# A hybrid state-space, attention and expert layer: the state-space group in chunks of four tokens, both token groups at once, weights read once

## What is computed

```python
sh1, sc1, g1, sh2, sc2, g2 = modulation(cvec, w_mod, b_mod)      # silu(c) @ w_mod, 12 pieces of 512
h = modulate(x, norm1, sh1, sc1)
u, c_q, c_kv, k_rope = split(h @ w_in)                            # 512, 384, 256, 32
# S5 group: 32 groups of 16 channels and 64 complex states, forward and backward
#   h_t = A h_{t-1} + B u_t   (A diagonal),   y_t = D u_t + Re(C h_t)
ssm_out, ssm_state = s5_mixer(u)          # gelu(y) * sigmoid(gelu(y) @ w_glu)
attn = attend(q, k, v)                    # 8 heads; group 1 also sees the cached latents
x = x + g1 * (concat([ssm_out, attn]) @ w_out)
h2 = modulate(x, norm2, sh2, sc2)
# experts: 8 heads, top 16 of 128 x 128 keys each -> 128 picks of 16384 rows per token
act = gelu(einsum('nd,nhkd->nhk', h2, u_table[idx])) * softmax(best)
x = x + g2 * einsum('nhk,nhkd->nd', act, v_table[idx])
```

## Time and profile before

| | |
|---|---|
| median of 3 runs | 947.65 us (945.67 to 949.99) |
| profiled execution, whole | 953.76 us |
| its span, first to last instruction | 952.0 us |
| TensorE, VectorE, ScalarE, POOL busy | 761.3, 632.1, 267.0, 427.5 us |
| mean granted TensorE clock | 0.896 of 2.4 GHz |
| moved by DMA | 339.02 MB, 356 GB/s over the span |

### The profile page before, as it was taken

The page is one execution under the profiler, slowest core; times in us unless marked ns, Lnnn a source line. Parts: engine busy times, 40 slices in busy tenths (PEclk is TensorE's granted clock), DMA queues, the critical chain, the costliest instruction groups (busy, mean ns, idle before and its releaser), DMA issues. The chain is left out here.

```text
span 952.0 us, 9512 instructions
## 1 busy us (share of the span) xinstructions
PE 761.3 (80%) x3129; PEld 396.9 (42%) x3129; DVE 632.1 (66%) x1327; ACT 267.0 (28%) x836; POOL 427.5 (45%) x380
## 2 busy tenths in 40 slices
PE   4798869656688999979998788876786888787885
PEld 0474534544344664336665533332332333333331
DVE  7689975684779737475853478469649756845453
ACT  3334451011245531213132224223222221311220
POOL 1058972556433344154344154653543635354520
PEclk9889789768799999989999898997988989788997
DMA  9937682067799999999999999999999999999991
GB/s 381 405 143 314 268 304 79 5 236 256 296 393 399 364 423 421 403 386 390 420 421 420 421 422 412 421 423 421 421 422 421 396 421 422 364 423 422 421 421 42
DMA packets 48250, 339.02 MB, mean 356 GB/s; under 512 B 5628, under 2 KB 6076, under 8 KB 8392
## 3 DMA queue, kind: packets, MB, share of 16 engines
q0 software_dynamic: 36864, 268.45, 68.8%
q1 hardware_dynamic: 10968, 69.78, 18.4%
q10 hardware_dynamic: 368, 0.18, 0.1%
HBM read 337.16 MB, written 1.23 MB: 355 GB/s over the span
## 5 line engine op out<-in xcount | busy, mean ns | idle before, releaser
L618 PE MATMUL psum<-mem 128*128 128x512 f32 x1024 | 489.8, 636 | 107.9 <-ACT mem L955 107.9
L1197 POOL DMA_INDIRECT mem<-uv_table,small x256 | 304.2, 1188 | 382.4 <-PE psum L618 330.8
L1504 DVE CUSTOM_DVE_ANT_0 mem<-mem,h 128x1024 f32<-128x1024 f32 x256 | 307.2, 1225 | 201.6 <-DMA mem<-uv_table,small 199.7
L618 PEld LDWEIGHTS psum<-mem 128*128 128x128 f32 x1024 | 205.1, 204 | 379.6 <-issue 253.4
L943 ACT ACTIVATE small<-small 128x4 f32<-128x4 f32 x64 | 13.1, 205 | 396.1 <-DVE small L1504 396.0
L955 ACT ACTIVATE mem<-consts,small 128x128 f32<-128x128 f32 x256 | 80.8, 386 | 0.0
L597 PEld LDWEIGHTS psum<-hT,mem 128*128 128x128 f32 x512 | 63.2, 205 | 4.2 <-issue 3.1
L597 PE MATMUL psum<-hT,mem 128*128 128x128 f32 x512 | 63.6, 289 | 0.7 <-issue 0.7
L1172 POOL TENSOR_TENSOR mem<-mem 128x512 f32<-128x512 f32 x32 | 46.1, 1460 | 39.7 <-DVE mem L1356 39.7
L1159 POOL TENSOR_TENSOR mem<-mem 128x512 f32<-128x512 f32 x32 | 50.1, 1574 | 22.3 <-DVE mem L1342 22.3
L948 ACT ACTIVATE small<-small 128x1 f32<-128x1 f32 x256 | 54.5, 283 | 5.9
(11 more groups left out here) (158 smaller groups left out, 604.5 us busy)
## 6 DMA issues: line engine op xcount, KB each, us to landing
mem<-w_mod SPq DMA_DIRECT2D x24, 1024.0 KB, 11.7
mem<-w_query SPq DMA_DIRECT2D x14, 1024.0 KB, 9.2
mem<-w_out SPq DMA_DIRECT2D x8, 1024.0 KB, 9.2
mem<-uv_table,small POOLq DMA_INDIRECT x256, 13.3
mem<-w_in_qkv SPq DMA_DIRECT2D x4, 1008.0 KB, 11.2
mem<-w_uq SPq DMA_DIRECT2D x4, 576.0 KB, 5.9
mem<-w_in_u SPq DMA_DIRECT2D x2, 1024.0 KB, 16.5
mem<-w_ukv SPq DMA_DIRECT2D x2, 1024.0 KB, 9.5
```

The source lines that it names most:

```text
L618: mm = pe.matmul(bank(f"acc_{g}_{half}"), diag[:, pick % DEEP, :], rows[pick % ROWS][:, D + 512 * half:D + 512 * half + 512], start=first ...
L1197: pool.indirect_dma_start(rows[row], None, uv_table, bass.IndirectOffsetOnAxis(ap=idx[:, pick:pick + 1], axis=0)).then_inc(row_landed[row] ...
L1504: dve.tensor_tensor_reduce(out=row[:, 0:D], in0=row[:, 0:D], in1=h[:, it // NB, :], scale=1.0, scalar=0.0, op0=ALU.mult, op1=ALU.add, accu ...
```

## The change

The state-space group is cut into chunks of four tokens. With powers of A multiplied into B and C beforehand (`xpow`, `ypow`), four tokens by 16 channels make a vector of 64: the input of 32 chunk states is one matmul 64 x 64 per block (`s5_in`), the scan runs over 33 steps instead of 128 (one is the initial state), and the output is the carried part (`y_carried`) plus what the chunk's own tokens give (`y_local`, with Toeplitz matrices from `kernels` and `toeplitz`). `shifted` brings tokens into chunk form, `y_spread` back. A unit now holds both groups, both directions and a quarter of the channels: 528 elements a partition, 4 units.

Both token groups now go through gate, projection inputs and latents together, and attention of group 1 up to its scores stands before the expert loop. qkv, glu, out and all query pages are sent once; uq and ukv twice as before. Modulation is sent by steps of 128 rows, and its last quarter (g2) in the expert loop. Rows are handed out by `row_plan`: four pages at first, a fifth from pick 4, seven from pick 6, nine from pick 25, eleven from pick 89.

```diff
-UN = 2 * NC
+STEP = 4
+CHUNKS = P // STEP
+SL = CHUNKS + 1
...
+PAGES = [(f"mod0.{k}", (0, 1, 2, 3, 4, 5, 0, 1)[k]) for k in range(8)]
+PAGES += [("in_u.0", 2), ("in_u.1", 3), ("qkv.0", 4), ("qkv.1", 5), ("qkv.2", 0), ("uq.0", 1), ("uq.1", 6), ("ukv", 7)]
+PAGES += [(f"mod1.{k}", (2, 3, 4, 5, 0, 2, 3, 4)[k]) for k in range(8)]
+PAGES += [("glu", 5), ("out0.0", 0), ("out0.1", 1), ("out1.0", 6), ("out1.1", 7)]
+PAGES += [(f"mod2a.{i}", (2, 3, 4, 2)[i]) for i in range(4)]
+PAGES += [("uq2.0", 3), ("uq2.1", 4), ("ukv2", 12), ("query0.0", 2), ("query0.1", 5), ("query1.0", 3), ("query1.1", 4),
+          ("query2.0", 2), ("query2.1", 5), ("query3.0", 3), ("query3.1", 4)]
+PAGES += [(f"mod2b.{i}", (2, 5, 2, 5)[i]) for i in range(4)]
...
+def row_plan():
+    free, arriving = [13, 14, 8, 9], {4: 15, 5: 0, 6: 1, 24: 6, 25: 7, 88: 3, 89: 4}
...
+        work = [mem[:, at_:at_ + WORK].rearrange("p (k n) -> p k n", k=4) for at_ in (Z0, Z0 + WORK, WIN0)]
+        BUF = (0, 1, 2, 0)
...
+            sp.wait_ge(coef_used, 1)
+            load("uq.1")
+            load("ukv")
+            for n in range(ORDER["mod1.0"], ORDER["uq2.0"]):
+                load(PAGES[n][0])
+                if PAGES[n][0] == "mod1.1":
+                    wait_filled(sp, "W_3_1")
+                    sp.wait_ge(x0_ready, 1)
+                    sp.dma_start(att[1].ckvn[:, 0, :], cache_ckv).then_inc(cache_in, 16)
+            load("uq2.0")
+            load("uq2.1")
+            sp.wait_ge(y_ready, NC)
+            sp.wait_ge(last_ready, 2 * NC)
+            load("ukv2")
+            sp.dma_start(n2b[0], norm2.to_broadcast([P, D])).then_inc(n2_in, 16)
+            sp.dma_start(page(10), keys).then_inc(keys_in, 16)
+            for name in ("query0.0", "query0.1", "query1.0", "query1.1"):
+                load(name)
+            wait_filled(sp, "mix_1_1")
+            sp.dma_start(n2b[1], norm2.to_broadcast([P, D])).then_inc(n2_in, 16)
+            for n in range(ORDER["query2.0"], len(PAGES)):
...
+            def input_weights(c):
+                if c == 0:
+                    pe.wait_ge(xpow_ready, 1)
+                for r in range(2):
+                    out = start(f"W_{c}_{r}")
+                    for a in range(8):
+                        for e in range(2):
+                            es = slice(64 * e, 64 * e + 64)
+                            mm = pe.matmul(out[es, 64 * a:64 * a + 64], xpow[es, r, 8 * c + a, :, :].rearrange("p k q -> p (k q)"),
+                                           ident[es, es], start=True, stop=True, tile_position=(64 * e, 64 * e))
...
+            def shifted(out, c, moving):
+                for j in range(4):
+                    for low in range(2):
+                        for e in range(2):
+                            for high in range(2):
+                                q = 64 * e + 32 * high
+                                mm = pe.matmul(out[q:q + 32, 64 * j:64 * j + 64], pad[:, 2 * j + e, 16 - 16 * low:48 - 16 * low],
+                                               moving(2 * high + low), start=low == 0, stop=low == 1, tile_position=(0, q))
+                return mm
...
+            def kernels():
...
+                for c in range(NC):
+                    for d, at_, lo, hi in ((0, 3, 0, 4), (1, 0, 2, 5), (1, 3, 5, 6)):
+                        for r in range(2):
+                            for j in range(4):
+                                a, o_ = 8 * c + 4 * d + j, 112 * c + SP_ * at_
+                                mm = pe.matmul(out[32 * j:32 * j + 32, o_:o_ + SP_ * (hi - lo)], x0[:, a, r, :],
+                                               ypow[:, r, a, lo:hi, :].rearrange("p k q -> p (k q)"),
+                                               start=c == 0 and d == 0 and r == 0, stop=c == NC - 1 and lo == 5 and r == 1,
+                                               tile_position=(0, 32 * j))
...
+            def toeplitz(half):
...
+                for c in range(2 * half, 2 * half + 2):
+                    mm = shifted(out[:, 256 * (c % 2):256 * (c % 2) + 256], c, lambda s: kern[:, c, 16 * (3 - s):16 * (3 - s) + 64])
+                finish(mm, f"m_{half}")
+
...
             def s5_in(u):
-                g, v = u // UN, u % UN
-                c, d = v // 2, v % 2
+                wait_emptied(pe, f"W_{u}_0")
+                wait_emptied(pe, f"W_{u}_1")
+                wait_emptied(pe, f"Us_{u}")
                 if u:
                     pe.wait_ge(bu_used, u)
                 for r in range(2):
-                    for j in range(4):
-                        mm = pe.matmul(psum[:, j, P * r:P * r + P],
-                                       fbT[32 * j:32 * j + 32, UN * r + v, :], tokens(uT[32 * j:32 * j + 32, g, c, :], d),
-                                       start=True, stop=True, tile_position=(32 * j, 0))
+                    for a in range(8):
+                        d, j = a // 4, a % 4
+                        for e in range(2):
+                            es = slice(64 * e, 64 * e + 64)
+                            mm = pe.matmul(psum[es, r, 64 * a:64 * a + 64], win[es, u, r, a, :],
+                                           chunks(ut[es, u, j, :].rearrange("p (g n) -> p g n", g=G), d),
+                                           start=True, stop=True, tile_position=(64 * e, 64 * e))
                 mm.then_inc(bu_ready, 1)
 
-            def s5_out(u):
-                g, v = u // UN, u % UN
-                c, d = v // 2, v % 2
+            def y_local(u):
+                wait_emptied(pe, f"m_{u // 2}")
+                if u >= 2:
+                    pe.wait_ge(y_read, u - 1)
+                out = psum[:, 4 + u % 2, :]
+                for j in range(4):
+                    for e in range(2):
+                        es = slice(64 * e, 64 * e + 64)
+                        pe.matmul(out[es, 64 * j:64 * j + 64], toep[es, u, j, :], ut[es, u, j, :], start=j == 0, stop=False,
+                                  tile_position=(64 * e, 64 * e))
+
+            def y_carried(u):
                 pe.wait_ge(qd_ready, 2 * u + 2)
                 pe.wait_ge(qp_ready, 2 * u + 2)
-                if u and d == 0:
-                    pe.wait_ge(y_read, u // 2)
-                for k, (r, b) in enumerate(((0, 0), (0, 2), (1, 1), (1, 3))):
+                out = psum[:, 4 + u % 2, :]
+                for j in range(4):
+                    for d in range(2):
+                        a = 4 * d + j
+                        for k, (r, b) in enumerate(((0, 0), (0, 2), (1, 1), (1, 3))):
+                            for e in range(2):
+                                es = slice(64 * e, 64 * e + 64)
+                                mm = pe.matmul(out[es, 64 * j:64 * j + 64], ypow[es, r, 8 * u + a, 1:5, :].rearrange("p k q -> p (k q)"),
+                                               chunks(view(u, b)[es, a, :, 0:CHUNKS], d),
+                                               start=False, stop=j == 3 and d == 1 and k == 3, tile_position=(64 * e, 64 * e))
+                mm.then_inc(y_ready, 1)
+
+            def y_spread(u):
+                pe.wait_ge(ysb_ready, u + 1)
+                out = psum[:, 4 + u % 2, 256:512].rearrange("p (g n t) -> p g n t", g=G, t=STEP)
+                for t in range(STEP):
                     for j in range(4):
-                        mm = pe.matmul(psum[32 * j:32 * j + 32, 4, P * c:P * c + P], cm[:, r, 4 * v + j, :],
-                                       tokens(work[:, u % 3, b, P * j:P * j + P], d),
-                                       start=d == 0 and k == 0, stop=d == 1 and k == 3, tile_position=(0, 32 * j))
-                mm.then_inc(q_used, 1)
+                        mm = pe.matmul(out[32 * j:32 * j + 32, :, :, t], phase[:, t, :],
+                                       ysb[:, u % 2, j, :], start=True, stop=True, tile_position=(0, 32 * j))
+                mm.then_inc(ysh_ready, 1)
 
...
+            def available(page_):
+                if page_ in (13, 14):
+                    pool.wait_ge(y_ready, NC)
+                    pool.wait_ge(last_ready, 2 * NC)
+                elif page_ in (8, 9):
+                    pool.wait_ge(h2_ready, 1)
+                elif page_ == 15:
+                    wait_filled(pool, "at1")
+                elif page_ in (0, 1):
+                    wait_filled(pool, f"mix_1_0")
+                elif page_ in (6, 7):
+                    pool.wait_ge(h2_ready, 2)
+                else:
+                    wait_filled(pool, "qry_1_3")
 
             def gather(pick):
-                row = pick % ROWS
                 if pick % BATCH == 0:
                     pool.wait_ge(idx_ready, pick // BATCH + 1)
-                if pick >= ROWS:
-                    pool.wait_ge(row_free, pick - ROWS + 1)
-                elif row < 2:
-                    wait_filled(pool, "mix_0_1")
-                elif row < 6:
-                    pool.wait_ge(qd_ready, 2 * UN + 4 * (row - 1))
```

(32 more changed lines are left out.)

1263 lines of the change are left out of this document (663 added, 600 removed), and 8 rows, old and new, of tables (LAST_USE, late).

## The result

The changed kernel takes **972.43 us** (median of 4 runs, 969.48 to 977.13); the kernel before took 947.09 in the same series (4 runs, 945.67 to 949.99). The ratio is 1.026, 95% interval 1.0231 to 1.0289: slower by 25 us, on the side and near the figure of the forecast (970). The profiled execution took 973.73 us, its span is 971.9, so 974 was forecast for it. Of all executions reported here one, the fourth of E6 (1029.54 us at a mean granted clock of 0.742), fell into a slower state and is left out of its median here.

What follows compares the result with a forecast made beforehand. The start of the gather stream, then bytes at 421 GB/s, queue idle and a tail were taken to set the time: 240 + 45 + 643 + 25 + 21 = 974 us span, 970 at the median's scale; range 933 to 998.

Steps and rivals of the forecast that it cites:

- S: End of the first score product on TensorE, the mark that closes the prelude; forecast at 240 us.
- Larger work: TensorE's larger matmuls and transposes from 40 us to the first score product: 118 us, between 111 and 125.
- Small work: 1,792 small matmul instructions before the first score product: 35 ns each, 62 us, bounds 30 and 122 us.
- Waits: TensorE's waits for other engines and pages before the first score product: 20 us in all.
- S to R: From the first score product to the first row handed back, through group 1's attention and output projection: 45 us.
- R: First row handed back, which lets gather 7 go; forecast at 285 us against 244 before.
- R to the end: After the first returned row: 643 us of bytes, 25 us of idle queues and 21 us of tail.
- About 13: Turn-round of seven rows up to pick 23: about 13 us for 4 picks against 9.96 of bytes.
- Small products by their columns: Rival: small matmuls before the first score product cost 17 ns, 30 us; median 938 us, faster; chance 0.22.
- Pairs that don't overlap: Rival: 960 small 64 x 64 instructions cost 68 instead of 35 ns, 32 us more; median 1001; chance 0.10.
- The wash: Rival: small matmuls go at the spacing of their starts, 25 ns, 45 us; median 953 us; chance 0.12.
- The third rival: Too few rows after the first returned row: idle 45 instead of 25 us, VectorE's finds; median 990; chance 0.10.

Runs made afterwards that it cites:

- E6: E4 with pages 0 and 1 named for gathers 9 and 10 instead of 5 and 6; 959.84 us, ratio 1.0142.
- E4: Changed kernel, group 1's keys behind first scores, its gate row and half its output projection in the softmax wait, accumulate(0) before the other half; 974.51 us.
- E8: E7 with three waits of TensorE's prelude filled by reordering work on VectorE, TensorE and ScalarE; 947.48 us, ratio 0.9984.
- E5: Changed kernel with small matmuls altered: (a) y_carried one half after the other, (b) 32 moving columns, (c) contiguous input shifts; 989.78 us, one execution.
- E10: Changed kernel with 14 more weight page loads, 14.68 MB, sent behind the final norm to unused pages; 1008.64 us, ratio 1.0621.
- E11: E8 with group 1's residual moved behind the second batch's products on VectorE; 941.68 us, ratio 0.9913.
- E7: E6 with norm 2 of group 1 two batches earlier, pages 6 and 7 rows from gather 16 instead of 24; 960.16 us, ratio 1.0116.
- E9: Changed kernel with 504 of y_carried's 512 instructions left out; 963.95 us, ratio 1.0171.
- E2: Changed kernel with accumulate(0) ahead of group 1's gate row and output projection; 984.88 us, ratio 1.041.

## Why the prediction was right

**S, the first score product: forecast 240, measured 224.6.** The trace splits it as the sum did: 40 + 111.0 of larger TensorE work + 50.3 of small + 23.3 idle.
- Larger work, "I take 118", was 111.0, the lower end of what I had bracketed, but not by the clock alone. I had taken the itemised 125 us to stand at the clock of the whole stretch, 0.85. Five of the nine items, 57 us, came out as priced: latents 1.13 us a step, output projection 14.1 (14.2 said), keys and values 10.7 (10.7), queries 8.2 (8.1), spread rows 5.9 (5.9). The rows that they were priced from ran at full clock already: 16 instructions of the output projection take 7.03 us before, and 7.03 at a granted clock of 1.00 now. Three fell: input projection 14.6 (18.5), gates, query block and scores 16.2 (20.9), modulation 15.4 (16.9). The rest came to 13 (12), and neighbouring groups overlap by 5. The new prelude ran at 0.98. So the step that failed here is one clock for all rows, and that the sum in the end hit one of its two bounds is partly luck.
- Small work, "I take 35 ns, 62 us", was 50.3 us for the 1,792 instructions, 28.1 ns; this term is the larger miss. No single price would do: kernels 11.9 ns (2.29 us for 192), Toeplitz matrices 15.6, y_spread 20, input shifts, s5_in and y_carried 30.5 to 33.
- Waits 20, measured 23.3. Of the list, the probabilities took 5.6 (6 said), key block 1 2.65 (2), the gelu 2.3 (3), mod2a.3 1.4 (2), the last h2 1.4 (2). Group 1's latents leaving their bank and y_evac(1), 2 each, cost nothing. Not on the list: the gaps ahead of 85, 89 and 92 us and one near 70, 6.2 us in all.

**S to R: 45, measured 47.8.** The find took 10.9 to the first gather (10.4 said). The order of waits was as forecast: gather 4 for at1, 5 and 6 for mix_1_0, 7 for R.

**R to the end: 643 + 25 + 21, measured 700.** Taken from the table of stretches at 421 GB/s, the bytes are 646 us, the tail is 20 to 21 (VectorE's last product starts at 951.58), and the idle is **33** instead of 25, 23 of it between 272 and 350 us. "About 13" for four picks on seven rows was too small: the gathers that the first returned row of a batch releases go at 272.35, 291.01 and 310.21, 19 us apart. I had priced one row's way round, and left out what stands ahead of each accumulation on TensorE:

```profile
277.15 1.98 PE L486 MATMUL psum<-modrow,consts 64*128 64x512 f32 x4
284.78 3.78 PE L486 MATMUL psum<-modrow,consts 128*128 128x512 f32 x4 [5.65 <-DVE mem L1512]
288.36 7.53 PE L746 MATMUL psum<-mem 128*128 128x512 f32 x16
299.21 9.01 PE L725 MATMUL psum<-hT,mem 128*128 128x128 f32 x64 [3.32 <-DVE mem L1521]
308.06 7.03 PE L746 MATMUL psum<-mem 128*128 128x512 f32 x16
```

ScalarE has the weights of the second batch ready at 281.7, but its accumulation (L746) starts at 288.36, behind the spread rows of norm 2 (L486), which wait 5.65 us until VectorE's residual has emptied a bank. Those of the third batch are ready at 300.7, and its accumulation starts at 308.06, behind a query block (L725). That is 7 us of each round. No run moved these two alone. E4 and E8 show the same kind of thing in kernels of mine, gathers standing behind an occupied page and products behind a residual; in the changed kernel itself gathers 5 and 6 go before any row is back, so the page does not hold it up.

So R was 12.7 us too late (S 15.4 too late, S to R 2.8 too short), the idle 8 and the bytes 3 too small: 974 against 971.9. That the figure is off by only 2 us is luck: errors of 12.7 and 11 us of opposite sign nearly cancel. With the measured larger and small work alone put into the sum, it gives 955 us, almost a wash; what made the change clearly slower besides them is what I had too short, the idle above all.

**The rivals.** Small products by their columns: against it E5 (b). At 17 ns they would have made the change faster by my sum; a quarter of them (kernels and Toeplitz matrices) were there, the rest not. Pairs that don't overlap: E5 (a) shows what that would cost, 28 ns an instruction. The wash (25 ns) was nearer to the measured price than I was: 28.1 against 25 and 35. The third rival, too few rows, was half true: idle 33, between 25 and 45, though by the rows above it was TensorE's order that held the pages up, and not VectorE's finds. The first gather, the mark that would have felled the forecast below 229, came at 235.5.

The Trainium skill (TensorE: Matmul & The Clock Gate, "Wait — 56ns, not 53.3ns?") has starts no closer than about 25 ns. The trace has 11.9 ns for the kernels, whose instructions go to four column strips in turn, on average 48 ns apart in each: across strips the measurement decides against the rule. The Trainium skill (TensorEngine Tiling (Array Packing), Key Properties) says that a change of tiling mode drains the engine. The trace agrees, and shows that it is short. Between two 64x64 groups the next one starts 0.17 us before the modelled end of the last (57.53 against 55.62 + 2.08); from the kernels in column strips to a 64x64 group it is 0.04 us (82.58 against 82.62), and from there to column strips 0.07 (86.33 against 86.40). So a change of form costs about 0.1 us, and thirty of them some 3 us (an estimate from these rows), a tenth of the 32 us that the rival had for pairs that don't overlap.

**What the change was worth, in parts.** By the spans, 971.9 against 952.0, it lost 20 us. Gather 7 goes 28 us later. From there to the end the queues' idle is 54 us instead of 39, the tail included, so 15 more (both tables of stretches, at 421 GB/s). The 9.7 MB less gain 23 (E10 shows that bytes there cost their full price). 28 + 15 - 23 is 20.

Was it the new arithmetic or the order? E11 keeps every new matmul and both groups at once, and is 31 us below the changed kernel by the order of work and of pages alone: 14 from E4 to E6 and 6 from E8 to E11 around the first rows, 13 from E7 to E8 in the prelude (what E4 itself did to the changed kernel, 2 us more, is within the noise). So the order is enough to undo the loss. That the arithmetic weighs less is not shown: leaving out 504 of the 1,792 small instructions was worth 8.5 us (E9), and no run left out the rest.

## To carry to other kernels

When the end is bound by a stream of transfers, look at the first buffers **handed back** as much as at the first transfer: E2 left the first gather where it was and lost 12 us, E11 left it within 1.2 us of E8 and gained 5.8. Read each in-order queue around that point for what stands in front without need: a gather on a page that is not free yet (14 us, E4 to E6), a residual in front of products (5.8 us, E8 to E11). And a batch of tiny matmuls has no one price: read spacing by tile form and by the stride of the moving operand.
